# A transformer block and a conformer block on one core: the stick-breaking softplus tail a step later on VectorE, its max on ScalarE, eleven modulation pieces moved to later steps

## The reference

```python
z = einsum('bqhd,bkhd->bhqk', q, k) * scale
past = kpos[None, :] < qpos[:, None]
log1m = where(past, -softplus(z), 0.0)
after = cumsum(log1m, reverse) - log1m
w = where(past, exp(log_sigmoid(z) + after), 0.0)
out = einsum('bhqk,bkhd->bqhd', w, v)
```

## Time and profile before

| | us |
|---|---|
| median of 3 runs (2645.72 to 2647.42) | 2645.82 |
| the profiled execution, its own time | 2647.79 |
| its span, first to last instruction | 2645.9 |
| PE busy | 2595.2 (98%) |
| PE weight loads busy | 2277.4 (86%) |
| DVE busy | 1874.5 (71%) |
| ACT busy | 1232.9 (47%) |
| POOL busy | 129.3 (5%) |

### The profile page before, as it was taken

The page is one execution under the profiler, slowest core; times in us unless marked ns, Lnnn a source line. Parts: engine busy times, 40 slices in busy tenths (PEclk is TensorE's granted clock), DMA queues, the critical chain, the costliest instruction groups (busy, mean ns, idle before and its releaser), DMA issues. The chain is left out here.

```text
span 2645.9 us, 40988 instructions
## 1 busy us (share of the span) xinstructions
PE 2595.2 (98%) x15425; PEld 2277.4 (86%) x15425; DVE 1874.5 (71%) x2655; ACT 1232.9 (47%) x1617; POOL 129.3 (5%) x203
## 2 busy tenths in 40 slices
PE   6999899999999999999999999999999999999998
PEld 4899898888888888888888888888888888888887
DVE  3468778887888888855666659999776644566554
ACT  3345544445645556544555541105554443444443
POOL 0021122001010000000000000000000000000000
PEclk8999999999999999999999999999999999999999
DMA  9998699768786877755666554554666655666554
GB/s 367 334 306 252 210 271 298 220 199 248 236 267 211 256 249 245 233 189 187 190 189 188 187 159 144 151 153 132 190 186 190 189 187 188 191 186 189 189 183 135
DMA packets 525076, 560.60 MB, mean 212 GB/s; under 512 B 20453, under 2 KB 487841, under 8 KB 524688
## 3 DMA queue, kind: packets, MB, share of 16 engines
q1 hardware_dynamic: 504448, 487.39, 58.1%
q0 software_dynamic: 20496, 71.38, 9.0%
HBM read 553.45 MB, written 2.10 MB: 210 GB/s over the span
## 5 line engine op out<-in xcount | busy, mean ns | idle before, releaser
L1126 DVE TENSOR_TENSOR wlo<-raw,whi 128x1024 fp32r<-128x1024 f32 x794 | 970.4, 1224 | 663.8 <-ACT whi L697 657.2
L697 ACT CAST whi<-raw 128x1024 fp32r<-128x1024 f32 x794 | 830.7, 1050 | 1037.1 <-PE ps L1944 896.5
L1942 PE MATMUL ps<-xhl,whi 128*128 128x512 f32 x3584 | 1130.6, 397 | 3.6 <-DVE xhl L1204 2.1
L1944 PEld LDWEIGHTS ps<-xhl,wlo 128*128 128x128 f32 x3584 | 674.3, 188 | 159.5
L1944 PE MATMUL ps<-xhl,wlo 128*128 128x256 f32 x3584 | 705.0, 278 | 0.0
L1942 PEld LDWEIGHTS ps<-xhl,whi 128*128 128x128 f32 x3584 | 547.0, 189 | 7.2 <-issue 5.1
L1942 PE MATMUL ps<-ghl,whi 128*128 128x512 f32 x1024 | 319.5, 393 | 0.0
L1944 PEld LDWEIGHTS ps<-ghl,wlo 128*128 128x128 f32 x1024 | 192.2, 188 | 44.5
L2304 PE MATMUL ps<-xg,raw 128*128 128x256 f32 x1024 | 221.5, 379 | 0.0
L1942 PE MATMUL ps<-fhl,whi 128*128 128x512 f32 x704 | 219.3, 392 | 0.0
L2304 PEld LDWEIGHTS ps<-xg,raw 128*128 128x128 f32 x1024 | 194.5, 190 | 26.4
(11 more groups left out here) (343 smaller groups left out, 2132.2 us busy)
## 6 DMA issues: line engine op xcount, KB each, us to landing
raw<-in_w_in SPq DMA_DIRECT2D x176, 512.0 KB, 4.9
raw<-in_w_up SPq DMA_DIRECT2D x176, 512.0 KB, 3.6
raw<-in_ffn_w_up SPq DMA_DIRECT2D x128, 512.0 KB, 3.7
raw<-in_ffn_w_down SPq DMA_DIRECT2D x128, 512.0 KB, 3.4
ada<-in_w_ada POOLq DMA_DIRECT2D x109, 512.0 KB, 4.9
raw<-in_w_down SPq DMA_DIRECT2D x88, 512.0 KB, 3.4
att<-in_w_ada SPq DMA_DIRECT2D x32, 1024.0 KB, 10.9
raw<-in_conv_w_pw SPq DMA_DIRECT2D x128, 256.0 KB, 3.2
```

What stands on the lines that cost most here:

```text
L697: nc.scalar.copy(whi[t % SPL][:, :, :], raw[t % RAW][:, :, :]).then_inc(s_hi, 1)
L1126: nc.vector.tensor_tensor(wlo[t % SPL][:, :, :], raw[t % RAW][:, :, :], whi[t % SPL][:, :, :].bitcast(F32), ALU.subtract).then_inc(s_lo, 1)
L1942: mm(o[:, m, :, :], whi[t % SPL][:, c, m * P:(m + 1) * P], x, start=first and c == 0, stop=last and c == KC - 1, skip_group_check=True)
L1944: ins = mm(o[:, m, 0, :], wlo[t % SPL][:, c, m * P:(m + 1) * P], x[:, 0, :], start=False, stop=last and c == KC - 1, skip_group_check=True)
```

## The change

Four edits, all in the order of instructions but one.

- On DVE the tail of the softplus (`tB + tA`, `tD`, the logs) moves from the even step of a head to its odd step, behind the split there. The max, `tB = max(z * scale, 0)`, moves from DVE to ACT, as a Relu with scale behind the Ln and ahead of the output copy. It waits for the suffix sum of the head before, which reads `tB`, and adds 1 to the semaphore that DVE waits for, `s_soft`.
- The odd steps from 25 to 41 hold no modulation piece any more, and the steps 30 and 36 hold one and not two. One more piece stands in each of the steps 43, 64, 66, 68, 70, 78, 80, 82, 84, 86 and 88.
- `read_first` of the first group of a pair is called at k = 3 of each ten units and not at k = 4.
- The first `read_modulation` goes from step 55 to step 63.

```diff
 def pieces_in(s):
-    if s < 15 or B_ROPE <= s < B_ROPE + 8 and s % 3 or ...
+    if s < 15 or B_STICK <= s < B_ROPE - 2 and s % 2 or B_ROPE <= s < B_ROPE + 8 and s % 3 or ...
         return 0
-    return 2 if s in (18, 19, 20, 22, 30, 36, 42, 52, 54, 56, 58, 87) else 1
+    return 2 if s in (18, 19, 20, 22, 42, 43, 52, 54, 56, 58, 64, 66, 68, 70, 78, 80, 82, 84, 86, 87, 88) else 1
...
                     nc.scalar.activation(tA[:, 0:384], tA[:, 0:384], ACT.Ln, bias=one_c[:, 0:1]).then_inc(s_soft, 1)
+                    if h:
+                        act.wait_ge(s_af, h)
+                    nc.scalar.activation(tB[:, 0:384], bank_z[:, 0:384], ACT.Relu, scale=SCALE).then_inc(s_soft, 1)
...
-                if k == 4:
+                if k == 3:
                     read_first(2 * j + 2)
...
-                if (s - B_STICK) % 2 == 0 and 0 <= h < HEADS:
-                    dve.wait_ge(s_soft, h + 1)
-                    sv.did(nc.vector.tensor_scalar(tB[:, 0:384], bank_z[:, 0:384], SCALE, 0.0, ALU.mult, ALU.max))
-                    sv.wait()
+                if (s - B_STICK) % 2 == 1 and 0 <= h < HEADS:
+                    dve.wait_ge(s_soft, 2 * h + 2)
                     sv.did(nc.vector.tensor_tensor(tB[:, 0:384], tB[:, 0:384], tA[:, 0:384], ALU.add))
...
-                if s == B_VTB + 3:
+                if s == B_ROPEI + 4:
                     read_modulation(ADA_START, ADA_START + 5)
```

More of the change, by code:

```diff
@@ L114, in pieces_in @@
 def pieces_in(s):
-    if s < 15 or B_ROPE <= s < B_ROPE + 8 and s % 3 or B_ROPEI <= s < B_ROPEI + 5 and s != B_ROPEI + 2 or B_IDX + 8 <= s < B_DSA:
+    if s < 15 or B_STICK <= s < B_ROPE - 2 and s % 2 or B_ROPE <= s < B_ROPE + 8 and s % 3 or B_ROPEI <= s < B_ROPEI + 5 and s != B_ROPEI + 2 or B_IDX + 8 <= s < B_DSA:
         return 0
-    return 2 if s in (18, 19, 20, 22, 30, 36, 42, 52, 54, 56, 58, 87) else 1
+    return 2 if s in (18, 19, 20, 22, 42, 43, 52, 54, 56, 58, 64, 66, 68, 70, 78, 80, 82, 84, 86, 87, 88) else 1
 def pieces_by(s):
```

## The result

| | before | after |
|---|---|---|
| median of 18 runs, us | 2647.65 | 2651.97 |
| range of these | 2645.72 to 2650.7 | 2649.06 to 2654.03 |
| the profiled execution, own time | 2647.79 | 2654.03 |
| its span | 2645.9 | 2652.2 |
| PE busy | 2595.2 | 2594.2 |

The ratio after / before is 1.0015, 95% interval [1.0008, 1.0021], which is 4.0 us: slower, by less than the 0.2% that the prediction counted as no change.

The account below looks back on a forecast made before the run. The prediction took TensorE (PE), busy 98% of the span, as the bound. Its terms, -4.6 - 3.3 + 0 + 4.8 + 3.5 = +0.4 us, on the median of 2645.82 gave 2646.2 us, range 2639.5 to 2653.0.

Parts of the forecast that it names:

- the rival in which VectorE falls behind in the indexer: Indexer steps: lateness from added pieces adds up and reaches PE at DSA's first transposes, +6.6 us, 2652.8; chance 0.13.
- the group's sum: Step 88, before the output projections: two pieces make PE wait 3.3 us, with clock loss +3.5 us, between +1.2 and +5.5.
- Everywhere else PE runs without a pause: Outside the stretches listed, PE was said not to wait, so work taken from DVE there is worth nothing.
- First read-out: First modulation, near 65 us: PE's wait and the clock fall behind it go, -4.6 us, between -1.6 and -5.0.
- The rival in which the clock falls anyway: First modulation: the clock falls at 67 us all the same, +3.0 us, 2649.2; chance 0.11.
- Stick heads: Stick steps: fewer pieces outweigh the moved softplus tail, PE's wait only moves; -3.3 us, between -9.1 and 0.
- stalls go altogether: Stick steps: all PE stalls vanish, -9.1 instead of -3.3 us, 2640.4; needs a loop below 13.97; chance 0.16.
- Indexer: Steps 64, 66, 68, 70: four added pieces hidden in DVE's idle time, 0 us; 6.6 if not.
- DSA: Steps 78 to 86 and behind: added pieces delay the chain of the shifted logits, +4.8 us, between 0 and +6.6.
- The rival in which DSA absorbs them: DSA: DVE's idle time there hides the added pieces, 0 instead of +4.8 us, 2641.4; chance 0.10.
- Pieces at 42 and 43, read at step 63: Pieces at 42 and 43 and the later modulation read-out: first user of the gate is far behind, 0 us.

Follow-up runs that it names:

- e1_first_only: The kernel before, with only the first read-out of a pair called at k = 3; 2644.65 us, ratio 0.9985 to before.
- e2_table_only: The kernel before, with only the new places of the modulation pieces and the read at step 63; 2649.59 us, ratio 1.0006 to before.
- e3_soft_only: The kernel before, with only the softplus edits (tail in the odd step, max on ScalarE); 2656.04 us, ratio 1.0027 to before.
- e5_room: The kernel before, with the early first read-out, read at step 63 and stick pieces moved to steps where DVE idled, softplus as before; 2634.98 us, ratio 0.9950.
- e9_room_dsa: `e5_room` with the second pieces of steps 65, 67 and 69 done in 78, 80 and 82; 2638.66 us, ratio 0.9963 to before.
- e10_room_three: `e5_room` with the second pieces of steps 65 and 67 done in 86 and 88; 2640.92 us, ratio 0.9970 to before.
- e11_room_one: `e5_room` with the second piece of step 87 done in 88; 2635.77 us, ratio 0.9952 to before.
- e8_room_relu: `e5_room` with the max on ScalarE but the softplus tail kept in the even step; 2634.47 us, ratio 0.9945 to before.
- e4_wab_off: The changed kernel, with the second pieces of steps 86 and 88 done in 65 and 67; 2646.33 us, ratio 0.9991 to before.
- e6_room_soft: `e5_room` with the whole softplus edit (tail in the odd step, max on ScalarE); 2640.18 us, ratio 0.9967 to before.
- e7_room_tail: `e5_room` with the softplus tail in the odd step but the max kept on DVE; 2642.00 us, ratio 0.9978 to before.

## Why the prediction was right in its range and where its sum was off

Forecast: 2646.2 us, +0.4 against before, range 2639.5 to 2653.0; measured: 2651.97, +4.0. Of the distance to 2646.2, 1.8 us is the kernel before, whose median was 2645.82 in three runs and 2647.65 in eighteen. In the trace, +6.3 stands against the +0.4. Five of six terms held within 2 us, one was three times too small. That the time lies in the range is in part luck: the upper end came from the rival in which VectorE falls behind in the indexer, which did not happen, while the term that did grow, the group's sum, went beyond its own bound (+5.5).

"Everywhere else PE runs without a pause" is not quite so. Before unit 26, PE also waits 15.6 us for DMAs; after the change it is 14.4, and these waits were no part of the sum.

1. *First read-out*: -4.6 forecast, -5.5 in the trace of the change, -4.0 us by itself at the end (`e1_first_only`). The wait is gone and the clock stays up. The rival in which the clock falls anyway is out: of the fourteen profiles the three with the 1.6 us wait (before, `e2_table_only`, `e3_soft_only`) have a granted clock below 1.00 behind it, the eleven without it have none there. The Trainium skill ("TensorE: Matmul & The Clock Gate", section "Why this matters for your kernels"), where it speaks of pauses, warns only of ones longer than this; here the measurement decides, and at this place, with eight one-column matmuls behind it, a pause of 1.6 us was enough. The term was 0.9 short, mainly because the other two blocks gave 0.3 and 0.5 us (units 16 and 26) where the prediction allowed 0.2 at most. The size of the clock's part was partly luck: the profile before has 6.9 us of the lower clock behind this wait, those of `e2_table_only` and `e3_soft_only` 3.5 and 3.6. By their price of 1.7 the term would be 1.6 + 1.7 + 0.8 = 4.1, an estimate that fits the -4.0 of `e1_first_only`.
2. *Stick heads*: -3.3 forecast, -5.1 in the trace, -4.1 without the modulation sum that only moved and that the prediction left out too. The mechanism is as told: the late cast (5.6 of 5.7), the loop (14.24 of 14.35), from the first to the last suffix add 101.3 us after 108.9 (-7.6 of -7.1), the wait that moves to z (5.4 of 7). In its parts the pieces gave -11.6 (`e2_table_only`) and the softplus +7.3 (`e3_soft_only`). What the prediction did not say is that PE would have been free without the softplus edit: the rival "stalls go altogether" names a loop below 13.97 as its condition, and the pieces alone reach it (97.2 us for seven loops in `e2_table_only`, 13.9 each).
3. *Indexer*: 0 forecast, +0.2 for the stretch; the slower rival, in which VectorE does not catch up there, is out, even with seven pieces more than before in 64 to 70 (`e5_room`: 1.0 us over all steps from 51 to 77, and this is the moved sum).
4. *DSA*: +4.8 forecast, +5.4 in the trace, 4.4 without the moved sum, and 4.1 for three pieces by themselves (`e9_room_dsa`, 4.9 forecast for three). The rival in which DSA absorbs them is out.
5. *The group's sum*: +3.5 forecast, +10.5 in the trace, and this is the step that failed. The prediction took one piece more (1.65), 0.2 for the three double steps, and 1.7 for the clock. It gave the lateness of the transfers as 0.2, since it looked at one transfer (4.1 us in the earlier trace rows) and not at the rate of two buffers: 7.0 us for a pair against 5.6 us of a step. Over the steps 86 to 88 that adds up to a wait of 6.4 (`e10_room_three`), where 88 alone has 2.8 (`e11_room_one`, 3.3 forecast). The changed kernel had 9.4; its last transfer took 7.3 us where the one before took 5.3, which makes 2 of the remaining 3. `e2_table_only`, with the same table of pieces, waited 7.3, so these 2 us differ between two profiles of the same order. That the steps 80 to 84 had two pieces as well may make the last 0.9; this was not tried apart. So the wait was 6.1 short. What the stretch lost beyond the longer wait is the clock's part: 10.5 - (9.4 - 1.5) = 2.6 in the changed kernel, 8.2 - (6.4 - 1.5) = 3.3 in `e10_room_three`, 2.8 - (2.8 - 1.5) = 1.5 in `e11_room_one`; 1.7 was forecast.
6. *Pieces at 42 and 43, read at step 63*: 0, as forecast.

A last +0.7 us lies far behind, where both kernels run the same instructions. The sum missed by 5.9 us in the trace and by 3.6 in the medians, less than its worst term, since two small misses of the other sign (-1.8 and -0.9) stood beside the large one (+7.0); had only the total been looked at, none of them would have been seen.

## What to carry to other kernels

Moving work out of a stretch where the follower engine sets the pace pays only if its new place has idle time that hangs on nothing in the same chain: the indexer's steps took seven more pieces for almost nothing, DSA's steps, though DVE stands idle for 1.3 to 2.5 us in each of 78 to 84, hid only 0.8 of 4.9 us. A stall on an engine is worth removing only if what it delays is asked for: here, once the pieces were gone, DVE's 3.45 us wait had 4.2 us of play behind it, and moving the work past it cost 5 to 7 us, because the result came too late for its reader and closed the loop. And a stream through n buffers has its own pace: a piece every (transfer plus use) / n, here 7.0 / 2 = 3.5 us against the 2.8 that a step with two pieces allows. Compare this with the demand of every run of busy steps, not with a single one.

## What the hardware showed

The granted clock fell behind some waits of PE and not behind others of the same length: the wait of 1.6 us for the group's sum in `e5_room` has none behind it, and the one of 1.5 us in `e8_room_relu` has one of 7.0 us, in this window:

```profile
628.00:640.00 12.00, 11.89 (x53) 10.45 (x54) 4.98 (x7) 5.28 (x7) 1.45 (x2) 0.72 0.68 232
```

That stretch costs +3.1 us against before in `e8_room_relu` and +0.1 in `e5_room`, and the profile of `e8_room_relu` is 2.1 us longer although its median is 0.5 lower. The early fall came back at half its length (about 3.4 us of low clock) in the profiles of `e2_table_only` and `e3_soft_only`, which both keep the 1.6 us wait ahead of it: they are 1.2 and 1.5 us ahead of before at unit 26 with no edit that acts there.

Nine of the fourteen profiles have a wait of 1.3 to 1.7 us ahead of this sum. Five of them (`e1_first_only`, `e3_soft_only`, `e4_wab_off`, `e8_room_relu`, `e9_room_dsa`) show the lower clock behind it and four (before, `e5_room`, `e6_room_soft`, `e7_room_tail`) don't, and no edit divides the two groups. Ahead of the first read-out the same length of wait had the fall in three of three. What makes the difference stays open.

So a clock term can be right in size and still be a chance from execution to execution. Profiles of single executions are not to be compared to better than some 3 us in this kernel: that of `e9_room_dsa` is 2.9 us above its own median, that of `e5_room` 2.3 below.
